# Four norm boundaries and an embedding stage, rebuilt around ScalarE evictions, pairs of tiles and squares kept off GpSimd

## The chip, the cores and the metric

The kernel runs on one core of a Trainium2 chip. The metric is the device time of one launch in microseconds (us), smaller is better. All tensors are float32; a product of float32 precision is made of three TensorE passes over operands that are split in a high and a low part.

## What is computed

Two blocks over 272 rows (16 meta rows and 256 tokens) and a model width of 2048: an attention layer and a pooling layer, then a second block with an RWKV-7 mixer beside a latent attention, a gated convolutional FFN and a gated embedding. Each sublayer ends in the same way, and this is the part that matters here:

```python
def rms_norm(x, g):
    xf = x.astype(jnp.float32)
    y = xf * lax.rsqrt(jnp.mean(xf * xf, axis=-1, keepdims=True) + RMS_EPS)
    return (y * g.astype(jnp.float32)).astype(x.dtype)
...
        h = h + rms_norm(y, post_norm_g[i])
...
        h = h + rms_norm_2(mix, post_mix_norm[i])
        u = rms_norm_2(h, pre_ffn_norm[i])
...
        h = h + rms_norm_2(f, post_ffn_norm[i])
        e = p[i] @ w_ple[i]
        h = h + rms_norm_2(jax.nn.sigmoid(h @ w_ple_gate[i]) * e, ple_norm[i])
```

The result drops the 16 meta rows, and after the pooling windows (up to 16 rows back) they are needed by nothing.

## The kernel before

Activations lie transposed in SBUF: 16 tiles of 128 channels by 256 or 272 rows (`h` the residual stream, `y` a sublayer's result, `xa` and `xb` the operands, each as a high and a low part). Weights come in 393 slots of 1 MB, four k-tiles by 512 columns each, through a ring of four raw buffers. Per slot SP issues one DMA once the slot four earlier is used (L229), ScalarE makes the high part in two halves (`split_hi`, L187), VectorE subtracts it for the low part (`split_lo`, L194), and TensorE runs 4 column tiles x 4 k-tiles x 3 passes = 48 matmuls (`products`, L210 to L212) into four PSUM banks. Four slots make a chunk of four output tiles; chunks go in turn to banks 0 to 3 and 4 to 7. The order of every engine's work is written out by hand: each engine runs one long queue, in order, with semaphore waits.

A *boundary* lies between an output projection (`attn_out`, `pool_out`, `mix_out`, 16 slots each, or the last four `down` slots of the FFN) and the projection that follows it. Before the change it goes so:

- In the projection (`y_stage_pe`, L309) VectorE copies each chunk of four tiles from PSUM to `y` (L331), ScalarE squares it (L323), VectorE adds the squares (L335).
- After the last chunk TensorE sums the squares over partitions with four matmuls by ones (`sum_squares`, L242), ScalarE takes the root (L249), VectorE the reciprocal (L691).
- `operands_dve` (L253) then goes through four groups of four tiles: y times the reciprocal (L258), four times h += gain * y (L261), four times the low part of the next operand (L271; L269 where no gain is applied). `operands_act` (L278) makes the high parts (L288, L286) in between, and GpSimd squares the new h and adds the squares up (`squares_pool`, L294, L300 to L304). Each group signals `x_ready`, which frees one slot of the next projection's first chunk (`first_chunk_pe`, L704). The weight splits of slots 2 and 3 stand behind groups 2 and 3.
- The second norm (of h, applied by scaling the results of the next projection) is summed by L242 behind the first chunk and rooted at once.

Boundary 1 is attn_out to pool_in, 2 is pool_out to rw_down, 3 is mix_out to the FFN. Boundary 4 is the FFN to ple_gate: there the two `ple` slots (the embedding, half a slot at a time) run between the FFN's last products and the gate's first, `e_taken` being ScalarE's evictions of them (L1829). The kernel ends with the norm of ple_gate's result (L1972 to L1978) and four output DMAs. In pool_in (32 slots at 272 columns), GpSimd forms the windowed means of each of four groups from the evictions of chunks 0 to 3 (L793 to L802) and ScalarE and VectorE wait for them in their queues between two weight splits (L759, L817).

## Time and profile before

| | us |
|---|---|
| median of 3 runs | 2834.61 (2830.41 to 2836.78) |
| the profiled execution | 2834.77, of which the trace spans 2833.0 |
| TensorE busy | 2597.2 (92% of the span) |
| VectorE busy | 1708.5 (60%) |
| ScalarE busy | 1134.5 (40%) |
| GpSimd busy | 214.4 (8%) |
| mean granted TensorE clock | 0.947 of full speed |
| granted clock from 957.5 to 959.5, after the wait in boundary 2 | 0.50 |
| the same from 989 to 991 | 1.00 |
| first pooling on GpSimd (L793 to L802) | 660.41 to 672.08, 11.7 us |

A row of a timeline gives start, duration, engine, source line, operation, tiles, shapes and count; in square brackets the idle time of that engine before it and who ended it. Consecutive instructions of one form are merged, with the duration of all of them. Matmuls overlap in the pipeline, so their own durations (0.28 us) are longer than their spacing (about 0.12 us); TensorE's time is best read from its idle gaps and from the spacing of what it releases.

### The profile page before, as it was taken

How to read it: one execution, taken by the hardware profiler on the slowest of the kernel's cores; microseconds unless marked ns; L12 is line 12 of the kernel's file. 1: busy time of each engine (PE TensorE's matmuls, PEld its weight loads, DVE VectorE, ACT ScalarE, POOL GpSimd, SP SyncE). 2: the span in 40 equal slices, each digit the busy share in tenths (PEclk: the TensorE clock that was granted, in tenths of full speed). 3: DMA queues.
4: the chain of work that ended last, by engine and by line, in shares of the span. 5: the costliest groups of instructions: out<-in, count | busy, mean ns of one | idle time of the engine just before them, and what ended most of it. 6: DMA issues, size and time to landing. Idle time of an engine off the chain costs nothing.

```text
span 2833.0 us, 52259 instructions
## 1 busy us (share of the span) xinstructions
PE 2597.2 (92%) x22498; PEld 2544.9 (90%) x22498; DVE 1708.5 (60%) x1909; ACT 1134.5 (40%) x1486; POOL 214.4 (8%) x117
## 2 busy tenths in 40 slices
PE   5999999879999787987998999998999999999986
PEld 5999999879999787886986999987999999999986
DVE  5565666566455786294363544558666666666664
ACT  3344445423344351241244333434444444444452
POOL 3000000014400231031000000002000000000000
PEclk9999999999999899798796999998999999999998
DMA  4444444334445341040140555553455555554442
GB/s 162 164 149 148 148 149 147 120 133 143 170 177 186 112 160 73 31 148 33 62 162 30 189 184 190 182 179 123 167 190 179 191 179 191 178 190 180 178 149 104
DMA packets 59618, 419.97 MB, mean 148 GB/s; under 512 B 6464, under 2 KB 8640, under 8 KB 9056
## 3 DMA queue, kind: packets, MB, share of 16 engines
q1 hardware_dynamic: 59280, 417.26, 41.0%
q8 instruction: 109, 1.79, 0.2%
q0 software_dynamic: 208, 0.75, 0.1%
q14 instruction: 21, 0.17, 0.0%
HBM read 415.89 MB, written 2.10 MB: 148 GB/s over the span
## 4 chain that ended last, share of the span: by engine, by line
PE 85%; DVE 10%; ACT 2%; POOL 1%; issue 1%; DMA 1%; SPq 0%; DVEq 0%; ACTq 0%; POOLq 0%
PE banks L210 25%; PE banks L212 25%; PE banks L211 25%; DVE xa_lo_sb L271 2%; DVE weights_lo_sb L194 2%; PE banks L242 1%; DVE h_sb L261 1%; PE banks L918 1%; PE banks L1006 1%; POOL rw_tile_sb L1159 1%; PE banks L996 1%; PE banks L1005 1%; DMA raw_weights_sb<-weights 1%; PE banks L1392 1%; PE banks L375 1%
## 5 line engine op out<-in xcount | busy, mean ns | idle before, releaser
L210 PE MATMUL banks<-xa_hi_sb,weights_hi_sb 128*128 128x256 f32 (+1 forms) x4800 | 1379.7, 287 | 80.0 <-DVE xa_lo_sb L271 29.9
L212 PE MATMUL banks<-xa_hi_sb,weights_lo_sb 128*128 128x256 f32 (+1 forms) x4800 | 1366.4, 285 | 0.0
L211 PE MATMUL banks<-xa_lo_sb,weights_hi_sb 128*128 128x256 f32 (+1 forms) x4800 | 1363.9, 284 | 0.0
L194 DVE TENSOR_TENSOR weights_lo_sb<-raw_weights_sb,weights_hi_sb 128x1024 fp32r<-128x1024 f32 x786 | 947.3, 1252 | 312.7 <-ACT weights_hi_sb L187 303.1
L187 ACT CAST weights_hi_sb<-raw_weights_sb 128x1024 fp32r<-128x1024 f32 x786 | 778.5, 1046 | 640.8 <-DMA raw_weights_sb<-weights 640.5
L210 PEld LDWEIGHTS banks<-xa_hi_sb,weights_hi_sb 128*128 128x128 f32 x4800 | 914.8, 191 | 88.5 <-issue 38.2
L211 PEld LDWEIGHTS banks<-xa_lo_sb,weights_hi_sb 128*128 128x128 f32 x4800 | 917.3, 191 | 0.5
L212 PEld LDWEIGHTS banks<-xa_hi_sb,weights_lo_sb 128*128 128x128 f32 x4800 | 915.1, 191 | 0.0
L210 PE MATMUL banks<-ff_hi_sb,weights_hi_sb 128*128 128x256 f32 x704 | 200.0, 284 | 2.7 <-DVE ff_lo_sb L1891 2.7
L211 PE MATMUL banks<-ff_lo_sb,weights_hi_sb 128*128 128x256 f32 x704 | 199.7, 284 | 0.0
L210 PE MATMUL banks<-xb_hi_sb,weights_hi_sb 128*128 128x256 f32 (+1 forms) x688 | 196.6, 286 | 2.7 <-DVE low_flat_sb L1517 1.3
L212 PE MATMUL banks<-ff_hi_sb,weights_lo_sb 128*128 128x256 f32 x704 | 198.0, 281 | 0.0
L212 PE MATMUL banks<-xb_hi_sb,weights_lo_sb 128*128 128x256 f32 (+1 forms) x688 | 196.0, 285 | 0.0
L211 PE MATMUL banks<-xb_lo_sb,weights_hi_sb 128*128 128x256 f32 (+1 forms) x688 | 195.7, 284 | 0.0
L210 PEld LDWEIGHTS banks<-ff_hi_sb,weights_hi_sb 128*128 128x128 f32 x704 | 132.4, 188 | 2.9 <-DVE ff_lo_sb L1891 2.9
L212 PEld LDWEIGHTS banks<-ff_hi_sb,weights_lo_sb 128*128 128x128 f32 x704 | 134.7, 191 | 0.0
L210 PEld LDWEIGHTS banks<-xb_hi_sb,weights_hi_sb 128*128 128x128 f32 x688 | 129.7, 189 | 3.6 <-DVE low_flat_sb L1517 1.5
L211 PEld LDWEIGHTS banks<-ff_lo_sb,weights_hi_sb 128*128 128x128 f32 x704 | 132.9, 189 | 0.0
L212 PEld LDWEIGHTS banks<-xb_hi_sb,weights_lo_sb 128*128 128x128 f32 x688 | 130.0, 189 | 0.0
L211 PEld LDWEIGHTS banks<-xb_lo_sb,weights_hi_sb 128*128 128x128 f32 x688 | 129.8, 189 | 0.1
L1917 DVE TENSOR_TENSOR y_sb<-y_sb,banks 128x1024 f32<-128x1024 f32 x40 | 48.9, 1222 | 47.6 <-PE banks L212 47.6
L271 DVE SCALAR_TENSOR_TENSOR xa_lo_sb<-h_sb,params_sb,xa_hi_sb 128x272 fp32r<-128x272 f32 (+1 forms) x64 | 66.9, 1107 | 0.4
(365 smaller groups left out, 2096.8 us busy)
## 6 DMA issues: line engine op xcount, KB each, us to landing
raw_weights_sb<-weights SPq DMA_DIRECT2D x393, 1024.0 KB, 4.8
h_sb<-h SPq DMA_DIRECT2D x1, 2176.0 KB, 8.6
out<-h_sb SPq DMA_DIRECT2D x4, 512.0 KB, 2.8
masks_sb<-consts_rw POOLq DMA_DIRECT2D x1, 352.0 KB, 4.8
params_sb<-params SPq DMA_DIRECT2D x1, 305.5 KB, 8.1
consts_first_sb<-consts_first SPq DMA_DIRECT2D x1, 304.0 KB, 9.2
ple_sb<-ple_in POOLq DMA_DIRECT2D x1, 256.0 KB, 3.0
consts_sb<-consts SPq DMA_DIRECT2D x1, 192.0 KB, 8.3
```

Source lines behind the costliest of these rows:

```text
L187: act.copy(c.w_hi[n % RAW][:, half], c.raw[n % RAW][:, half]).then_inc(c.sem("hi_done"), 1)
L194: dve.tensor_tensor(c.w_lo[n % RAW][:, half], c.raw[n % RAW][:, half], c.w_hi[n % RAW][:, half].bitcast(F32), ALU.subtract).then_inc(c.sem ...
L210: pe.matmul(out, w_hi[:, k, a], x_hi[:, tile, cols], start=begin, stop=False)
L211: pe.matmul(out, w_hi[:, k, a], x_lo[:, tile, cols], start=False, stop=False)
L212: done = pe.matmul(out, w_lo[:, k, a], x_hi[:, tile, cols], start=False, stop=end)
L242: m = pe.matmul(c.ps[:, bank, 0:n], c.const("ones"), acc[:, j, cols], start=j == 0, stop=j == 3)
L261: m = dve.scalar_tensor_tensor(out=c.h[:, k, cols], in0=t["tmp"][:, j, cols], scalar=c.param(g_post, k), in1=c.h[:, k, cols], op0=ALU.mult ...
L271: m = dve.scalar_tensor_tensor(out=c.xa[1][:, k, cols], in0=c.h[:, k, cols], scalar=c.param(g_pre, k), in1=c.xa[0][:, k, cols].bitcast(F32 ...
L375: m = pe.matmul(ps[0:b - a, 4 + comp, SCORES_AT[q]:SCORES_AT[q] + b], t["qk"][:, comp, a:b], t["qk"][:, 2 + comp, 0:b], start=True, stop=True)
L918: m = pe.matmul(ps[:, bank + j // 2, 256 * (j % 2):256 * (j % 2) + 256], ones, src[:, j, :], start=True, stop=True)
L996: m = pe.matmul(ps[at_[q], g, 64 * (u % 8):64 * (u % 8) + 64], t["lm"][at_[q], u, :], t["yy"][at_[q], u, :], start=True, stop=True)
L1917: dve.tensor_tensor(y, y, out(x), ALU.add).then_inc(S("down_taken"), 1)
```

## The change

Boundaries 1 to 4 and the end are rewritten. ScalarE instead of VectorE takes chunks out of PSUM, with the post-norm's gain applied in the same copy (`gained`), and squares straight from PSUM. The last chunk is taken by single tiles, each signalled by `tile_done` in the last slot; two of its six sum matmuls are put before that slot (`y_sums_begin_pe`). The boundary then runs over eight pairs of tiles: scale a pair, add it to h, high parts, low parts, and TensorE waits per half slot. The squares of the new h are ScalarE's, added up by VectorE (`h_squares_dve`) behind the first split of the following chunk and summed on TensorE after that chunk's first slot. The splits of the next projection's slots 2 and 3 stand earlier in both queues. GpSimd's squares go, except at the kernel's start. At boundary 4 the order of embedding evictions, root and splits on ScalarE changes. Pool_in's chunks 4 to 7, the group products and what follows them run on 256 rows instead of 272.

```diff
     for half in range(2):
         pe.wait_ge(c.sem("lo_done"), at(2 * n + half + 1, i, 2 * step))
+        if ready is not None:
+            pe.wait_ge(c.sem("x_ready"), ready + half + 1)
...
+            if each and half and j < 3:
+                done.then_inc(c.sem("tile_done"), 1)
     done.then_inc(c.sem("slot_used"), 1)
...
+def boundary_dve(c, dve, st, t, b, norm, cols, g_pre, splits):
+
+    dve.wait_ge(c.sem("root_done"), norm + 1)
+    st.did(dve.reciprocal(t["rs"][:, cols], t["sd"][:, cols]))
+    done = PAIRS * (b - 1)
+
+    def scaled(q):
+        yq = c.y[:, 2 * q:2 * q + 2, cols]
+        dve.tensor_tensor(yq, yq, wide(t["rs"][:, cols], 2), ALU.mult).then_inc(c.sem("y_scaled"), 1)
+
+    def updated(q):
+        hq = c.h[:, 2 * q:2 * q + 2, cols]
+        dve.wait_ge(c.sem("y_scaled"), done + q + 1)
+        dve.tensor_tensor(hq, hq, c.y[:, 2 * q:2 * q + 2, cols], ALU.add).then_inc(c.sem("h_ready"), 1)
+
+    def low(q):
+        dve.wait_ge(c.sem("x_hi_ready"), KT * b + 2 * q + 2)
+        pair = slice(2 * q, 2 * q + 2)
+        if g_pre is None:
+            m = dve.tensor_tensor(c.xa[1][:, pair, cols], c.h[:, pair, cols], c.xa[0][:, pair, cols].bitcast(F32), ALU.subtract)
+        else:
+            for k in range(2 * q, 2 * q + 2):
+                m = dve.scalar_tensor_tensor(out=c.xa[1][:, k, cols], in0=c.h[:, k, cols], scalar=c.param(g_pre, k),
+                                             in1=c.xa[0][:, k, cols].bitcast(F32), op0=ALU.mult, op1=ALU.subtract)
+        m.then_inc(c.sem("x_ready"), 1)
+
+    scaled(0)
+    updated(0)
+    for q in range(1, PAIRS):
+        scaled(q)
+        low(q - 1)
+        updated(q)
+        if q in splits:
+            split_lo(c, dve, splits[q])
+    low(PAIRS - 1)
+
...
+def h_squares_dve(c, dve, st, b, cols):
+
+    four = lambda g: c.y[:, 4 * g:4 * g + 4, cols]
+    for g in range(1, 4):
+        dve.wait_ge(c.sem("h_squared"), PAIRS * (b - 1) + 2 * g + 2)
+        st.did(dve.tensor_tensor(four(0), four(0), four(g), ALU.add))
+    dve.tensor_tensor(c.y[:, 0:2, cols], c.y[:, 0:2, cols], c.y[:, 2:4, cols], ALU.add).then_inc(c.sem("squares_ready"), 1)
+
+
+def boundary_act(c, act, b, cols, g_pre, splits):
+
+    for q in range(PAIRS):
+        act.wait_ge(c.sem("h_ready"), PAIRS * (b - 1) + q + 1)
+        for k in range(2 * q, 2 * q + 2):
+            if g_pre is None:
+                m = act.copy(c.xa[0][:, k, cols], c.h[:, k, cols])
+            else:
+                m = act.activation(c.xa[0][:, k, cols], c.h[:, k, cols], ACT.Copy, scale=c.param(g_pre, k))
+            m.then_inc(c.sem("x_hi_ready"), 1)
+        if g_pre is not None:
+            act.activation(c.y[:, 2 * q:2 * q + 2, cols], c.h[:, 2 * q:2 * q + 2, cols], ACT.Square).then_inc(c.sem("h_squared"), 1)
+        if q in splits:
+            split_hi(c, act, splits[q])
...
+def h_sums_pe(c, pe, cols, squares):
+
+    pe.wait_ge(c.sem("squares_ready"), squares)
+    for bank, a, part in spare(cols):
+        for j in range(2):
+            m = pe.matmul(c.ps[:, bank, a:a + part.stop - part.start], c.const("ones"), c.y[:, j, part], start=j == 0, stop=j == 1)
+    m.then_inc(c.sem("stats_done"), 1)
...
+def first_chunk_pe(c, pe, n0, x, b, cols):
+
+    for s in range(4):
+        products(c, pe, n0 + s, x, [(k, 4 * s + k) for k in range(4)], banks(c, 0, cols.stop - cols.start), cols,
+                 s == 0, s == 3, ready=x_before(b) + 2 * s)
...
+Y_SQUARED, Y_ADDED = 7, 3
+
+
+def y_sums_begin_pe(c, pe, t, base, cols, bank, a):
+
+    pe.wait_ge(c.sem("y_added"), Y_ADDED * (base // 4) + 3)
+    for j in range(2):
+        pe.matmul(c.ps[:, bank, a:a + cols.stop - cols.start], c.const("ones"), t["acc"][:, j, cols], start=j == 0, stop=False)
+
+
+def y_sums_end_pe(c, pe, t, base, cols, bank, a):
+
+    for j in range(4):
+        pe.wait_ge(c.sem("y_squared"), Y_SQUARED * (base // 4) + 3 + j + 1)
+        m = pe.matmul(c.ps[:, bank, a:a + cols.stop - cols.start], c.const("ones"), t["sq"][:, j, cols], start=False, stop=j == 3)
+    m.then_inc(c.sem("stats_done"), 1)
...
+            if chunk == s == 3:
+                pe.wait_ge(c.sem("y_taken"), base + 3)
+                y_sums_begin_pe(c, pe, t, base, cols, 0, 0)
...
+                     banks(c, chunk % 2, cols.stop - cols.start), cols, s == 0, s == 3,
+                     ready=None if ready is None or chunk else ready + 2 * s, each=chunk == s == 3)
+    y_sums_end_pe(c, pe, t, base, cols, 0, 0)
...
+def gained(c, act, chunk, j, cols, g_post, src):
+
+    k = 4 * chunk + j
+    return act.activation(c.y[:, k, cols], src, ACT.Copy, scale=c.param(g_post, k))
...
+    if chunk == 2:
+        act.wait_ge(c.sem("y_added"), Y_ADDED * (base // 4) + 1)
+    if chunk < 3:
+        act.wait_ge(c.sem("slot_used"), done)
+        act.activation((t["sq"] if chunk else t["acc"])[:, :, cols], c.ps[:, half:half + 4, 0:n], ACT.Square).then_inc(c.sem("y_squared"), 1)
+        for j in range(4):
+            m = gained(c, act, chunk, j, cols, g_post, bank(j))
+        m.then_inc(c.sem("y_taken"), 1)
+        return
+    act.wait_ge(c.sem("y_added"), Y_ADDED * (base // 4) + 2)
+    for j in range(4):
+        if j < 3:
+            act.wait_ge(c.sem("tile_done"), 3 * (base // 4) + j + 1)
+        else:
+            act.wait_ge(c.sem("slot_used"), done)
+        act.activation(t["sq"][:, j, cols], bank(j), ACT.Square).then_inc(c.sem("y_squared"), 1)
+        if j < 2:
+            gained(c, act, chunk, j, cols, g_post, bank(j))
+    for j in range(2, 4):
+        m = gained(c, act, chunk, j, cols, g_post, bank(j))
+    m.then_inc(c.sem("y_taken"), 1)
+
+
+def y_add_dve(c, dve, chunk, cols, base, t):
+
+    if chunk not in (1, 2):
+        return
+    count = Y_ADDED * (base // 4)
+    dve.wait_ge(c.sem("y_squared"), Y_SQUARED * (base // 4) + chunk + 1)
+    dve.tensor_tensor(t["acc"][:, :, cols], t["acc"][:, :, cols], t["sq"][:, :, cols], ALU.add).then_inc(c.sem("y_added"), 1)
+    dve.wait_ge(c.sem("y_added"), count + chunk)
+    if chunk == 2:
+        dve.tensor_tensor(t["acc"][:, 0:2, cols], t["acc"][:, 0:2, cols], t["acc"][:, 2:4, cols], ALU.add).then_inc(c.sem("y_added"), 1)
...
+        if n0 + m < N_SLOTS:
+            split(n0 + m)
         if m == 17:
             take(3, n0 + 16)
-        if n0 + m < N_SLOTS:
-            split(n0 + m)
-        if m % 4 == 1 and m < 17:
+        elif m % 4 == 1:
             take((m - 5) // 4, n0 + m - 1)
...
-        chunk(n0 + 12, 1, 2, i)
+            products(c, pe, n + s, c.xa, [(k, 4 * s + k) for k in range(4)], banks(c, half, cols.stop - cols.start), cols,
+                     s == 0, s == 3, i, 8)
+            if sums and s == 0:
+                h_sums_pe(c, pe, cols, 2)
+
+    chunk(n0 + 4, 1, None, R, sums=True)
+    chunk(n0 + 8, 0, 1, R)
+    chunk(n0 + 12, 1, 2, R)
+    with pe.Fori(0, 2) as i:
+        chunk(n0 + 16, 0, 3, BOTH, i)
+        chunk(n0 + 20, 1, 4, BOTH, i)
...
+    y_stage_split(c, lambda n: split_hi(c, act, n), lambda chunk, n: y_take_act(c, act, chunk, n, R, 0, t, "post0"), n0, 4)
+    root(c, act, 0, t["sd"], R, S("stats_done"), 2, S("root_done"))
+    split_hi(c, act, n0 + 18)
+    boundary_act(c, act, 1, R, "pre1", {1: n0 + 19})
...
 
     S = c.sem
     R = slice(0, ROWS)
-    squares_pool(c, pool, st, 1, R, t["acc"], t["sq"])
...
+        if m == 4:
+            h_squares_dve(c, dve, st, 1, R)
+        if m == 6:
             pre_root_dve(c, dve, st, t, 2, R)
-        if m % 4 == 1:
+        if m % 4 == 1 and m > 5 or m == 6:
             chunk = (m - 5) // 4
-            dve.wait_ge(S("slot_used"), n0 + m - 1)
+            dve.wait_ge(S("slot_used"), n0 + 4 * chunk + 4)
...
     masks, _ = columns(CONSTS_RW)
     mask = lambda name, k=16: wide(t["masks"][:, masks[name][0]:masks[name][1]], k)
     half = lambda x: ps[:, x:x + 2, :].rearrange("p b (j r) -> p (b j) r", j=2)
-    for m in range(4, 6):
-        split_lo(c, dve, n + m)
+    split_lo(c, dve, n + 4)
+    h_squares_dve(c, dve, st, 2, BOTH)
+    split_lo(c, dve, n + 5)
...
+        down(n, x, each=x == 3)
+    pe.wait_ge(S("tile_added"), 1)
+    y_sums_begin_pe(c, pe, t, 12, BOTH, 4, SEQ)
+    y_sums_end_pe(c, pe, t, 12, BOTH, 4, SEQ)
...
     pe.wait_ge(S("y_taken"), 15)
     ple(0, 0, 0)
     pe.wait_ge(S("y_taken"), 16)
+    pe.wait_ge(S("root_done"), 8)
     ple(0, 1, 1)
     pe.wait_ge(S("e_taken"), 1)
-    norm_between_pe(c, pe, t, 12, BOTH, 7)
+    ple(1, 0, 0)
     pe.wait_ge(S("e_taken"), 2)
-    ple(1, 0, 1)
-    pe.wait_ge(S("root_done"), 8)
-    ple(1, 1, 0)
+    ple(1, 1, 1)
     n = FIRST_SLOT["ple_gate"]
-    pe.wait_ge(S("e_taken"), 4)
-    y_stage_pe(c, pe, n, c.xa, BOTH, 16, lambda s: pe.wait_ge(S("x_ready"), 17 + s))
-    norm_between_pe(c, pe, t, 16, BOTH, 8)
+    pe.wait_ge(S("e_taken"), 3)
+    y_stage_pe(c, pe, t, n, c.xa, BOTH, 16, lambda s: pe.wait_ge(S("x_ready"), x_before(4) + 2 * s), ready=x_before(4))
...
+    for x in range(3):
         split_hi(c, act, n + 2 + x)
-        squares(x, 12)
+        taken(x)
+    split_hi(c, act, n + 5)
+    act.wait_ge(S("y_added"), Y_ADDED * 3 + 2)
+    for j in range(4):
+        if j < 3:
+            act.wait_ge(S("tile_added"), j + 1)
+        else:
+            act.wait_ge(S("y_taken"), 16)
+        act.activation(t["sq"][:, j, BOTH], c.y[:, 12 + j, BOTH], ACT.Square).then_inc(S("y_squared"), 1)
+    act.wait_ge(S("y_squared"), Y_SQUARED * 4)
+    for j in range(4):
+        gained(c, act, 3, j, BOTH, "post_ffn", c.y[:, 12 + j, BOTH]).then_inc(S("y_gained"), 1)
+    root(c, act, 4, t["sd"], BOTH, S("stats_done"), 8, S("root_done"), at=SEQ)
     n = FIRST_SLOT["ple"]
 
     def e_taken(x, half):
         act.wait_ge(S("slot_used" if x % 2 else "ple_done"), n + x // 2 + 1 if x % 2 else x // 2 + 1)
         act.copy(t["e"][:, 4 * x:4 * x + 4, :], c.ps[:, 4 * half:4 * half + 4, 0:SEQ]).then_inc(S("e_taken"), 1)
 
+    split_hi(c, act, n + 2)
     e_taken(0, 0)
+    split_hi(c, act, n + 3)
     e_taken(1, 1)
-    root(c, act, 0, t["sd"], BOTH, S("stats_done"), 8, S("root_done"))
-    e_taken(2, 1)
-    split_hi(c, act, n + 2)
-    e_taken(3, 0)
-    split_hi(c, act, n + 3)
+    boundary_act(c, act, 4, BOTH, None, {})
+    e_taken(2, 0)
...
-    for m in range(4, 6):
-        split_lo(c, dve, n + m)
+    split_lo(c, dve, n + 4)
+    h_squares_dve(c, dve, st, 3, BOTH)
+    split_lo(c, dve, n + 5)
+    split_lo(c, dve, n + 6)
     pre_root_dve(c, dve, st, t, 6, BOTH)
     dve.wait_ge(S("zeros"), 3)
     taken(0, 0, None, n + 4)
-    split_lo(c, dve, n + 6)
...
+    for x in range(3):
         split_lo(c, dve, n + 2 + x)
         dve.wait_ge(S("slot_used"), n + x + 1)
         y = c.y[:, 4 * x:4 * x + 4, BOTH]
         dve.tensor_tensor(y, y, out(x), ALU.add).then_inc(S("y_taken"), 1)
-        squares(x, 12)
+        y_add_dve(c, dve, x, BOTH, 12, t)
+    split_lo(c, dve, n + 5)
+    for j in range(4):
+        if j < 3:
+            dve.wait_ge(S("tile_done"), 3 * 3 + j + 1)
+        else:
+            dve.wait_ge(S("slot_used"), n + 4)
+        y = c.y[:, 12 + j, BOTH]
+        dve.tensor_tensor(y, y, ps[:, 4 + j, 0:SEQ], ALU.add).then_inc(S("tile_added" if j < 3 else "y_taken"), 1)
     n = FIRST_SLOT["ple"]
-    dve.wait_ge(S("root_done"), 8)
-    st.did(dve.reciprocal(t["rs"][:, BOTH], t["sd"][:, BOTH]))
     split_lo(c, dve, n + 2)
-    split_lo(c, dve, n + 3)
+    dve.wait_ge(S("y_gained"), KT)
+    boundary_dve(c, dve, st, t, 4, 7, BOTH, None, {3: n + 3})
...
+            else:
+                for j in range(4):
+                    y = c.y[:, 12 + j, BOTH]
+                    dve.wait_ge(S("ple_gated"), 3 + j + 1)
+                    dve.tensor_tensor(y, y, t["e"][:, 12 + j, :], ALU.mult).then_inc(S("tile_added"), 1)
+                    dve.wait_ge(S("tile_added"), 3 + j + 1)
+                    dve.tensor_tensor(t["sq"][:, j, BOTH], y, y, ALU.mult).then_inc(S("y_squared"), 1)
     dve.wait_ge(S("root_done"), 9)
...
+    done = 4 * PAIRS
+    for q in range(PAIRS + 1):
+        if q < PAIRS:
+            dve.wait_ge(S("y_gained"), KT + 2 * q + 2)
+            yq = c.y[:, 2 * q:2 * q + 2, BOTH]
+            dve.tensor_tensor(yq, yq, wide(t["rs"][:, BOTH], 2), ALU.mult).then_inc(S("y_scaled"), 1)
+        if q:
+            hq = c.h[:, 2 * q - 2:2 * q, BOTH]
+            dve.wait_ge(S("y_scaled"), done + q)
+            dve.tensor_tensor(hq, hq, c.y[:, 2 * q - 2:2 * q, BOTH], ALU.add).then_inc(S("out_ready"), 1)
```

## Rows read from the trace of the kernel before

**Rows 1.** TensorE's waits by releaser: us in total, times, longest.

```profile
PE banks L210 <- DVE xa_lo_sb L271: 29.9, 6, 9.2
```

**Rows 2.** The chain that ended last, boundaries 1 to 3: start, us, what.

```profile
601.46 1.30 DVE y_sb L331
...
654.78 1.83 PE banks L242 x8
...
940.35 1.24 DVE y_sb L331
...
991.82 1.73 PE banks L242 x8
...
1902.45 1.24 DVE y_sb L331
...
1952.09 1.73 PE banks L242 x8
```

**Rows 3.** TensorE's timeline at the first product of boundary 2.

```profile
955.96 0.58 PE L210 MATMUL banks<-xa_hi_sb,weights_hi_sb 128*128 128x256 f32 x1 [8.66 <-DVE xa_lo_sb L271]
```

**Rows 4.** VectorE's timeline in boundary 2.

```profile
947.85 1.75 DVE L691 RECIPROCAL rs_mid_sb<-sd_mid_sb 128x256 f32<-128x256 f32 x1 [1.54 <-ACT sd_mid_sb L249]
949.63 1.23 DVE L258 TENSOR_TENSOR tmp_sb<-y_sb,rs_mid_sb 128x1024 f32<-128x1024 f32 x1
950.89 1.67 DVE L261 SCALAR_TENSOR_TENSOR h_sb<-tmp_sb,params_sb,h_sb 128x256 f32<-128x256 f32 x4
...
958.79 5.46 DVE L271 SCALAR_TENSOR_TENSOR xa_lo_sb<-h_sb,params_sb,xa_hi_sb 128x256 fp32r<-128x256 f32 x4
...
972.46 2.35 DVE L194 TENSOR_TENSOR weights_lo_sb<-raw_weights_sb,weights_hi_sb 128x1024 fp32r<-128x1024 f32 x2
```

**Rows 5.** GpSimd's timeline in boundary 2, then GpSimd's and VectorE's at the kernel's start.

```profile
958.90 2.13 POOL L300 TENSOR_TENSOR sq_sb<-h_sb 128x1024 f32<-128x1024 f32 x1 [4.06 <-DVE h_sb L261]
...
24.59 3.35 POOL L304 TENSOR_TENSOR p_sb<-p_sb,a_sb 128x1088 f32<-128x1088 f32 x1
...
29.01 5.03 DVE L271 SCALAR_TENSOR_TENSOR xa_lo_sb<-h_sb,params_sb,xa_hi_sb 128x272 fp32r<-128x272 f32 x12
```

**Rows 6.** ScalarE's timeline: high parts of boundary 2, then boundary 4.

```profile
951.41 1.71 ACT L288 ACTIVATE xa_hi_sb<-h_sb,params_sb 128x256 fp32r<-128x256 f32 x4 [3.60 <-DVE h_sb L261]
...
2676.78 1.06 ACT L1820 ACTIVATE late_acc_sb<-y_sb 128x1024 f32<-128x1024 f32 x1 [6.68 <-DVE y_sb L1952]
2677.75 1.99 ACT L187 CAST weights_hi_sb<-raw_weights_sb 128x1024 fp32r<-128x1024 f32 x2
...
2699.60 1.28 ACT L249 ACT_TABLE_LOAD   x1
2700.89 0.48 ACT L249 ACTIVATE sd_sb<-banks,small_sb 128x256 f32<-128x256 f32 x1
```

**Rows 7.** VectorE's timeline in pool_in and at the first RWKV chunk.

```profile
750.69 1.29 DVE L817 TENSOR_TENSOR xb_lo_sb<-sq_sb,xb_hi_sb 128x1088 fp32r<-128x1088 f32 x1 [11.55 <-ACT xb_hi_sb L759]
...
777.66 1.29 DVE L830 TENSOR_TENSOR y_sb<-banks,rs_mid_sb 128x1088 f32<-128x1088 f32 x1 [3.72 <-PE banks L212]
...
801.85 1.29 DVE L830 TENSOR_TENSOR y_sb<-banks,rs_mid_sb 128x1088 f32<-128x1088 f32 x1 [3.68 <-PE banks L212]
...
1016.25 1.22 DVE L896 TENSOR_TENSOR y_sb<-banks,rs_sb 128x1024 f32<-128x1024 f32 x1 [1.89 <-PE banks L212]
```

**Rows 8.** VectorE's and TensorE's timeline at boundary 4.

```profile
2675.53 1.22 DVE L1952 TENSOR_TENSOR y_sb<-y_sb,banks 128x1024 f32<-128x1024 f32 x1 [2.94 <-PE banks L212]
...
2693.05 1.21 DVE L1952 TENSOR_TENSOR y_sb<-y_sb,banks 128x1024 f32<-128x1024 f32 x1
...
2714.80 0.55 PE L210 MATMUL banks<-xa_hi_sb,weights_hi_sb 128*128 128x256 f32 x1 [8.80 <-DVE xa_lo_sb L269]
```

**Rows 9.** ScalarE's timeline at the end, then VectorE's.

```profile
2807.43 1.02 ACT L1846 ACTIVATE y_sb<-banks 128x1024 f32<-128x1024 f32 x1 [15.39 <-PE banks L212]
...
2828.06 1.67 DVE L1978 SCALAR_TENSOR_TENSOR h_sb<-late_tmp_sb,params_sb,h_sb 128x256 f32<-128x256 f32 x4
```

313 lines of the change are left out of this document (136 added, 177 removed).

## The prediction

> **What bounds the kernel now.** The table comes first: TensorE is busy 92% of the span and no other engine over 60%, so what counts is where TensorE idles. The list of its waits names the place: its longest entry that the change touches is products that wait for the low part of an operand, L271, 29.9 us in six waits [rows 1]. They lie in boundaries 1 to 3. The chain of waits shows what one boundary costs: from the copy of the last chunk out of PSUM to the end of the second norm's sums, where the next projection's second chunk starts, pass 55.2, 53.2 and 51.4 us in boundaries 1, 2 and 3 [rows 2]. The work in it is one chunk: 24.2 us at 272 columns, the spacing of two evictions in pool_in [rows 7], and 22.5 us at 256, as from 991.82 + 1.73 to the next chunk's eviction at 1016.25 [rows 2, 7]. So each boundary holds some 30 us that are not products. They begin with 15.6 us before the first product of boundary 2 [rows 2, 3].
>
> In that stretch VectorE's rows show two kinds of time. Four updates of h (L261) take 1.67 us, four low parts (L271) of the same size 5.46 us [rows 4]. GpSimd squares h meanwhile [rows 5]. At the kernel's start, with GpSimd done at 27.94, twelve L271 at 272 columns take 5.03 us, 0.42 us each [rows 5]. So I take L271 alone at 0.42 us, and 1.37 beside GpSimd's squares.
>
> **Boundary 2, step by step** (0 is the copy's old start, 940.35; VectorE works at 1.23 us for four tiles, so 0.65 for a pair [rows 4]; ScalarE at 0.43 per tile [rows 6]). The last tile's square is ready at 0.5, its sum on TensorE at 1.8, as three of the four tail matmuls (0.43 each, 1.73 for four [rows 2]) wait for nothing. ScalarE copies the remaining tiles until 1.4 and then loads the root's table, 1.28 [rows 6], root at 3.2. Reciprocal (1.75 [rows 4]) 5.0; scale, add 6.4; two high parts 7.4; two low parts 8.3. First product at 8.4 instead of 15.6. From there a pair costs VectorE 0.65 (add) + 1.0 (ScalarE's high parts with two handovers, the next scale hidden in it) + 0.84 = 2.5 us, and TensorE 2.8 for its half slot. The two splits (2.35 each [rows 4]) cost VectorE about 3.2 net; TensorE has lead enough to lose only 1.4 of it. Then 22.5 of products and 1.5 for the clock, which is granted at half of full speed (1.2 of 2.4 GHz) for some 3 us after the idle time, as now (table): the second chunk starts at 8.4 + 22.5 + 1.5 + 1.4 = 33.8 instead of 53.2. Gain 19.4.
>
> What it gives back. Two sum matmuls now run before the last slot, two more inside the second chunk: 0.86 each time. The squares of h move to VectorE: three adds and a short one, 4.4 us behind the first split. Root and reciprocal come 6.7 us later than before relative to the second chunk. Behind them are queued the first shift, the split of the chunk's third slot (TensorE stalls 1.6 there), the angles and two more splits. VectorE then gets to the next eviction (before: 22.7 after the chunk's start, with 1.9 of slack [rows 7]) at 27.5, 4.8 late, and from there the chain runs over VectorE and GpSimd. Net of boundary 2: 19.4 - 0.9 - 4.8 = 13.7.
>
> **Boundary 1** by the same steps at 272 columns, no table load on the path (none stands there now): second chunk at 34.6, gain 20.6. Given back: 0.9 and 0.9 for sums. Its first eviction now waits for the later reciprocal, ends 12.2 after the chunk's start and only then releases GpSimd's pooling, for which ScalarE and VectorE wait in their queues before the split of slot 8. Pooling took 11.7 (table) and loses an instruction, I take 10.4; high and low part 2.3, half a split 1.2: the split is ready at 26.3, TensorE wants it at 25.1, stall 1.2. The fourth pooling ends in front of slot 20, today just in time (L817 ends at 751.98 [rows 7], chunk 5 starts at 753.2); with chunk 4 1.6 us shorter it costs 0.9. Net: 20.6 - 1.8 - 2.1 = 16.7.
>
> **Boundary 3**: second chunk at 33.8 instead of 51.4, gain 17.6. Back: 0.9 and 0.9 for sums, and 1.0 because the conv taps (later reciprocal) stand before the split of slot 7. Net 14.8. GpSimd's memset of y moves behind the sums and delays the first eviction to 12; it is hidden by chunk 2.
>
> **Pool gate.** 20 slots at 256 columns instead of 272: 24.2 against 22.5 for four [rows 7, 2], 0.41 a slot, TensorE being gapless there: -8.1. VectorE's group loop keeps up, since group 2 needs group 0 only.
>
> **Boundary 4** goes the other way. The FFN's last chunks are still added by VectorE, and now ScalarE multiplies each by its gain before the next split: add 1.3, square 1.1, four gains 1.7, split 2.0, then VectorE's low half 1.2, a period of 7.4 us [rows 4, 6] against TensorE's 5.7 for a slot. With the first add at 2675.5 [rows 8] the third ends at 2691.9, and the split of the second embedding slot stands before the single-tile adds: they start at 2698.2, while the products end at 2692.8, just ahead of today's last add [rows 8]. TensorE waits 5.8 us for the first of them and sums at half rate until 2703.2; gains, table load and root end at 2703.9. VectorE splits a slot (to 2707.3), takes the reciprocal (to 2709.1), and its first update of h ends at 2710.5. The products now wait for the third embedding eviction (`e_taken` 3), which is queued on ScalarE behind all eight pairs. So no pair overlaps a product: seven pairs at 2.25 (low part in one instruction, no square), 2.0 for a split and the last high parts end at 2729.2, the eviction at 2730.3, first gate product at 2730.4 against 2714.80 now [rows 8], where nothing stalls behind it either. Cost 15.6. The nearest rows bound it: 0 if the pairs overlapped as today, and 22 if the late adds came on top in full.
>
> **The end.** Now 25.6 us from the last eviction to the span's end, 22.3 of them until VectorE's last instruction at 2829.73 [rows 9]. After: last sigmoid 0.5, product and square 1.5, sum 2.3, root 2.9 (its table load hidden), reciprocal 4.7, sixteen pair operations of 0.65, 15.1. Gain 7.2, less 0.9 for the early sums: 6.4 rounded.
>
> **Sum.** 16.7 + 13.7 + 14.8 + 8.1 - 15.6 + 6.4 = 44.1. The profiled execution took 2834.77, the median is 2834.61: 2790.6.
>
> **A rule weighed.** The load of ScalarE's table took 1.28 us and the root began 0.01 us after it [rows 6]. The Trainium skill (ScalarE: Activation LUTs, What ACT_TABLE_LOAD costs) adds about 1.38 us of drain to each switch. By it the three switches on the path would take 4.1 us of the gain. The trace does not show it here, and the sum goes by the row.
>
> **Rivals.**
> 1. *A switch costs more than its row.* In boundaries 2, 3 and 4 the load is now on the path and nothing hides it. If it were twice its row, 3 x 1.3 are lost: 2794.5. Against it: root right behind the load [rows 6]. 6%. The rule above would put it so.
> 2. *The embedding boundary does overlap.* If the chain before it does not drift, or the eviction comes early, boundary 4 costs 0 to 5: 2777. Against it stands the queue order in the diff. 12%.
> 3. *The low parts stay slow*, because of the place (operands that ScalarE has just written) and not GpSimd. For it: 5.46 was measured at this place only; against it the 5.03 for twelve at the start, after ScalarE's writes too [rows 4, 5]. Then a pair costs 2.5 + 1.9 = 4.4 in boundaries 1 to 3, TensorE follows at that pace, 13 us lost in each: 2830. If the pairs of boundary 4 were slowed too by 1.9, 15 more are lost: 2845, slower than before. The point from which this decides is 1.6 us more per pair in all four. 4%.
> 4. *The splits fall behind.* ScalarE's four single copies per chunk come between weight splits in four projections. They are hidden by the ring (two slots, 11.3 us, are split ahead; the added work is 1.7). If that cover were gone, up to 1.7 x 12 = 20 come back: 2811. 6%.
> 5. *The change doesn't do what it says*: the second norm's root, late in all three places, sets new stalls beyond the 3.1 + 4.8 that I count. Twice as much: 2799. 12%.
>
> The forecast as it stands has 60%. Its own range is 2781 to 2801, from 3 us either way in each of three boundaries and 6 in boundary 4. To leave out no more than 2 in 10, I take in rivals 1, 2 and 5: 2775 to 2806. Within 0.2% of before (5.7 us, about what a measurement of this kernel can tell from no change) lie parts of rival 3 only.
> Faster 94%, same 3%, slower 3%.
>
> **What would show it.** L271's successor at 0.42 us a tile and no GpSimd work in boundaries 1 to 3: right on the cause. The chain from last product to second chunk of about 34 us in each. A TensorE gap before ple_gate of 13 to 16 us, released by ScalarE's embedding copy, and one of about 5.5 us before the FFN's sums. Stalls of 1 to 2 us at pool_in's slots 8 and 20, at the third slot of the first RWKV chunk, and of 1.0 at the FFN's slot 7. The prediction is wrong if the gate's gap is under 5 us, if pairs take over 2.9 us, or if new waits stand in the output projections.

## The result and the profile after

| | before | after |
|---|---|---|
| median, us | 2832.51 of 4 runs (2825.78 to 2836.78) | 2785.83 of 4 runs (2785.44 to 2786.22) |
| profiled execution, span | 2834.77, 2833.0 | 2786.22, 2784.4 |
| mean granted TensorE clock | 0.947 | 0.952 |
| VectorE, ScalarE, GpSimd busy | 1708.5, 1134.5, 214.4 | 1656.0, 1178.5, 163.0 |

The ratio is 0.9843, with an interval of 0.9824 to 0.9861: 46.7 us, 1.6% faster. The forecast was 2790.6, from 2775 to 2806.

TensorE's waits by releaser (total, times, longest), kernel after; they answer to [rows 1]:

```profile
PE banks L210 <- DVE xa_lo_sb L320: 18.9, 3, 6.5
PE banks L210 <- ACT e_sb L1957: 13.6, 1, 13.6
...
PE banks L210 <- DVE weights_lo_sb L194: 10.5, 6, 4.2
```

The 29.9 us for low parts are 18.9, one wait in each of boundaries 1 to 3; a new one of 13.6 stands at boundary 4. The waits for weight splits fell as well. The same view of the kernel before has:

```profile
PE banks L210 <- DVE weights_lo_sb L194: 25.2, 8, 4.2
```

Of these 25.2 us, 19.5 are six waits inside the first chunks of boundaries 1 to 3, two in each, and all six are gone. TensorE's timeline, kernel after, at all places that the prediction names:

```profile
610.19 0.57 PE L210 MATMUL banks<-xa_hi_sb,weights_hi_sb 128*128 128x272 f32 x1 [5.99 <-DVE xa_lo_sb L320]
...
733.39 0.39 PE L210 MATMUL banks<-xa_hi_sb,weights_hi_sb 128*128 128x256 f32 x1 [0.69 <-DVE weights_lo_sb L194]
...
923.34 0.55 PE L210 MATMUL banks<-xa_hi_sb,weights_hi_sb 128*128 128x256 f32 x1 [6.45 <-DVE xa_lo_sb L320]
...
953.79 1.02 PE L373 MATMUL banks<-y_sb,consts_sb 128*128 128x256 f32 x4
...
961.99 0.39 PE L210 MATMUL banks<-xa_hi_sb,weights_hi_sb 128*128 128x256 f32 x1 [1.54 <-DVE weights_lo_sb L194]
...
1870.86 0.55 PE L210 MATMUL banks<-xa_hi_sb,weights_hi_sb 128*128 128x256 f32 x1 [6.45 <-DVE xa_lo_sb L320]
...
1901.65 1.03 PE L373 MATMUL banks<-y_sb,consts_sb 128*128 128x256 f32 x4
...
1914.79 0.39 PE L210 MATMUL banks<-xa_hi_sb,weights_hi_sb 128*128 128x256 f32 x1 [0.83 <-DVE weights_lo_sb L194]
...
2611.06 0.58 PE L210 MATMUL banks<-ff_hi_sb,weights_hi_sb 128*128 128x256 f32 x1 [2.75 <-DVE ff_lo_sb L2035]
...
2642.23 2.08 PE L406 MATMUL banks<-late_acc_sb,consts_sb 128*128 128x256 f32 x4 [5.26 <-DVE y_sb L2100]
...
2672.89 0.58 PE L210 MATMUL banks<-xa_hi_sb,weights_hi_sb 128*128 128x256 f32 x1 [13.59 <-ACT e_sb L1957]
```

The first product of boundary 2 stood at 955.96 [rows 3], that of the gate at 2714.80 [rows 8]. L373 sums the squares of h one slot (5.66 us) into the second chunk, so that chunk starts at 948.1 and 1896.0. In boundary 1 the chain of waits of the kernel after has `642.40 1.18 PE banks L373 x8`; the chunk starts a slot of 272 columns (6.05) before it, at 636.35.

Where boundary 2 goes, ScalarE's and VectorE's timelines, kernel after (against [rows 4, 6]):

```profile
915.20 0.38 ACT L458 ACTIVATE sq_sb<-banks 128x256 f32<-128x256 f32 x1 [0.32 <-PE banks L212]
915.48 0.83 ACT L436 ACTIVATE y_sb<-banks,params_sb 128x256 f32<-128x256 f32 x2
916.33 1.28 ACT L251 ACT_TABLE_LOAD   x1
917.63 0.47 ACT L251 ACTIVATE sd_mid_sb<-banks,small_sb 128x256 f32<-128x256 f32 x1
...
922.32 0.88 DVE L320 SCALAR_TENSOR_TENSOR xa_lo_sb<-h_sb,params_sb,xa_hi_sb 128x256 fp32r<-128x256 f32 x2 [0.38 <-ACT xa_hi_sb L352]
...
924.77 0.88 DVE L320 SCALAR_TENSOR_TENSOR xa_lo_sb<-h_sb,params_sb,xa_hi_sb 128x256 fp32r<-128x256 f32 x2 [0.37 <-ACT xa_hi_sb L352]
```

Two low parts take 0.88 us instead of half of 5.46, and one pair follows another in 2.45 us. From the start of the last tile's square, straight from PSUM (915.20), 8.14 us pass to the first product and 32.9 to the second chunk.

The shift of the kernel after against the kernel before, stage by stage, adds up to the whole difference of the two profiled executions. The start of the last chunk's copy before [rows 2] answers to the last tile's square after (602.40, 915.20 and 1862.72 in boundaries 1 to 3). The last column is what the prediction let each step add to the shift; it adds up to its 44.1.

| point | before | after | shift so far | expected of this step |
|---|---|---|---|---|
| last copy, boundary 1 | 601.46 | 602.40 | +0.9 | +0.9 |
| second chunk of pool_in | 656.61 | 636.35 | -20.3 | -20.6 |
| last copy, boundary 2 | 940.35 | 915.20 | -25.2 | gate -8.1; +3.9 of sums and stalls |
| second chunk behind it | 993.55 | 948.1 | -45.5 | -19.4 |
| last copy, boundary 3 | 1902.45 | 1862.72 | -39.7 | +4.8, +0.9 |
| second chunk of the FFN | 1953.82 | 1896.0 | -57.8 | -17.6 |
| FFN's last down products | 2667.97 | 2611.06 | -56.9 | +1.9 |
| gate's first product | 2714.80 | 2672.89 | -41.9 | +15.6 |
| end of the span | 2833.0 | 2784.4 | -48.6 | -6.4 |

### The profile page after: what moved, and what is told of

Its sections match the earlier page's. It is cut to its first block, busy times and chain, and to the rows that moved or that the text cites. A ratio compares the mean times of both kernels' runs of the same rounds, so it can differ in the third digit from the quotient of the medians.

```text
span 2784.4 us, 52335 instructions
## 1 busy us (share of the span) xinstructions
PE 2580.3 (93%) x22510; PEld 2530.2 (91%) x22510; DVE 1656.0 (59%) x1891; ACT 1178.5 (42%) x1605; POOL 163.0 (6%) x92
## 3 DMA queue, kind: packets, MB, share of 16 engines
q8 instruction: 112, 1.84, 0.3%
## 4 chain that ended last, share of the span: by engine, by line
PE 85%; DVE 9%; ACT 3%; POOL 2%; issue 1%; DMA 0%; SPq 0%; DVEq 0%; ACTq 0%; POOLq 0%
PE banks L210 26%; PE banks L212 25%; PE banks L211 25%; DVE weights_lo_sb L194 3%; PE banks L1113 1%; PE banks L1024 1%; POOL rw_tile_sb L1265 1%; PE banks L1103 1%; PE banks L1112 1%; PE banks L1499 1%; PE banks L513 1%; PE banks L526 0%; PE banks L1498 0%; PE banks L1150 0%; PE banks L1161 0%
## 5 line engine op out<-in xcount | busy, mean ns | idle before, releaser
L210 PE MATMUL banks<-xa_hi_sb,weights_hi_sb 128*128 128x256 f32 (+1 forms) x4800 | 1374.2, 286 | 60.4 <-DVE xa_lo_sb L320 18.9
L2014 DVE TENSOR_TENSOR up_gate_sb<-banks,rs_sb 128x1024 f32<-128x1024 f32 x11 | 13.5, 1224 | 87.9 <-PE banks L212 86.3
```

Source lines behind the costliest of these rows:

```text
L210: pe.matmul(out, w_hi[:, k, a], x_hi[:, tile, cols], start=begin, stop=False)
```

## The experiments

Each starts from the kernel after unless it says otherwise. The runs of one kernel spread by up to 12 us here (15 in one case). A stretch of 900 us without any edit differs by up to 10 us between the profiled executions (last section), so small edits are read from their own stretch of the trace.

### GpSimd's squares put back (e1)

```diff
+    idle_squares_pool(c, pool, st, 2, BOTH, t["acc"], t["sq"])
...
+        pool.wait_ge(c.sem("h_ready"), PAIRS * (b - 1) + 2 * kg + 2)
+        st.did(pool.tensor_tensor((sq if kg else acc)[:, :, cols], hk, hk, ALU.mult))
+        if kg:
+            st.did(pool.tensor_tensor(acc[:, :, cols], acc[:, :, cols], sq[:, :, cols], ALU.add))
```

> The changed kernel with GpSimd's squares and adds of h put back at the first three boundaries, their result thrown away; nothing else waits for them. Theory (low parts are slow beside GpSimd): two low parts (L320, 0.88 us in the changed kernel) take 1.9 us more while GpSimd works, the pair's cycle goes from 2.45 to about 4.3 us against TensorE's 2.8 for half a slot, the four slots of the first chunk end 9 to 13 us later at each of the three boundaries: 27 to 39 us slower in all, near 2817. Rival (the slow low parts of the kernel before came from their place between updates, not from GpSimd): L320 stays at 0.88 us and the time within 2 us of 2785.8.

Measured: 2815.56 us, ratio to before 0.9932 (0.9908 to 0.9957), 29.7 slower than the kernel after. VectorE's and GpSimd's timeline in boundary 2:

```profile
940.89 0.87 DVE L320 SCALAR_TENSOR_TENSOR xa_lo_sb<-h_sb,params_sb,xa_hi_sb 128x256 fp32r<-128x256 f32 x2
...
942.51 2.21 POOL L340 TENSOR_TENSOR sq_sb<-h_sb 128x1024 f32<-128x1024 f32 x1 [5.69 <-DVE h_sb L311]
943.34 4.14 DVE L320 SCALAR_TENSOR_TENSOR xa_lo_sb<-h_sb,params_sb,xa_hi_sb 128x256 fp32r<-128x256 f32 x2 [0.38 <-ACT xa_hi_sb L362]
944.80 2.40 POOL L342 TENSOR_TENSOR acc_sb<-acc_sb,sq_sb 128x1024 f32<-128x1024 f32 x1
947.41 0.68 DVE L311 TENSOR_TENSOR h_sb<-h_sb,y_sb 128x512 f32<-128x512 f32 x1
```

The same two instructions, one pair later, take 4.14 us instead of 0.87 because they meet both GpSimd operations: they end at 947.48, the second of those at 947.20. So it is GpSimd and not the place, and rival 3 of the prediction is out. From TensorE's early sums to the second chunk, the three boundaries take 10.1, 11.1 and 9.3 us longer than in the kernel after: 30.5, which is all that the medians show.

### The kernel before without that load on GpSimd (e2)

```diff
+        cols = slice(cols.start, cols.start + 16) if b else cols
         hk = c.h[:, 4 * kg:4 * kg + 4, cols]
```

> The kernel before with GpSimd's squares of h cut to 16 columns at the first three boundaries (the second norm's sums are then of 16 columns only), all else as it was. Theory: the low parts of four tiles (L271, 5.46 us with GpSimd beside them) fall to about 1.7 us, four groups of them take 12 to 14 us out of VectorE's chain at each boundary, and the second chunk starts 10 to 14 us earlier: 30 to 42 us faster than the kernel before, near 2797, so that most of what the change brings is there without its other parts. Rival (the order by groups of four holds the boundary back, GpSimd is a side matter): 0 to 10 us faster.

Measured: 2791.97 us, ratio 0.9853 (0.9828 to 0.9878): the interval covers the 0.9843 of the whole change. Timelines of boundary 2 (against [rows 3 to 5]):

```profile
940.54 1.71 DVE L271 SCALAR_TENSOR_TENSOR xa_lo_sb<-h_sb,params_sb,xa_hi_sb 128x256 fp32r<-128x256 f32 x4
940.65 0.53 POOL L301 TENSOR_TENSOR acc_sb<-h_sb 128x64 f32<-128x64 f32 x1 [203.30 <-DVE h_sb L261]
...
942.31 0.58 PE L210 MATMUL banks<-xa_hi_sb,weights_hi_sb 128*128 128x256 f32 x1 [7.06 <-DVE xa_lo_sb L271]
```

Four low parts take 1.71 us instead of 5.46. The waits for weight splits behind the first product are gone too. In the kernel before TensorE's timeline has:

```profile
973.82 0.36 PE L210 MATMUL banks<-xa_hi_sb,weights_hi_sb 128*128 128x256 f32 x1 [3.61 <-DVE weights_lo_sb L194]
...
984.41 0.36 PE L210 MATMUL banks<-xa_hi_sb,weights_hi_sb 128*128 128x256 f32 x1 [3.18 <-DVE weights_lo_sb L194]
```

So these splits were late only because they stood behind the slow low parts in VectorE's queue. The gate's first product, 2714.80 before, came at 2670.76 here, 44.0 us earlier. Of these, 35.6 lie in the three boundaries, from TensorE's sums to the second chunk (12.8, 11.8 and 11.1). Another 6.3 lie in the stretch from boundary 2's second chunk to boundary 3's sums, 906.6 us instead of 912.9, which varies by more than that without any edit (last section). This kernel keeps groups of four, VectorE's copies and the gate's 272 columns. It also adds less than a full second norm needs, so I take 36 as the upper end for what leaving GpSimd brings, and the 30 that e1 gives back in the new order as the lower.

### The embedding copies moved inside (e3)

```diff
-    boundary_act(c, act, 4, BOTH, None, {})
-    e_taken(2, 0)
-    e_taken(3, 1)
+    boundary_act(c, act, 4, BOTH, None, {}, {0: lambda: e_taken(2, 0), 2: lambda: e_taken(3, 1)})
...
+        if q in after:
+            after[q]()
```

> The changed kernel with ScalarE's third and fourth copy of the embedding products moved from behind all eight pairs of the fourth boundary to behind its first and its third pair. Theory (the gate's first product waits 13.6 us for the third copy alone, and its operands have long been there): the gate starts 11 to 14 us earlier and all of it reaches the end, near 2773. Rival (the next wait takes its place: the raw weights of the gate's slots, which ScalarE waits 9.1 us for behind the stall): 0 to 5 us gained, near 2783.

Measured: 2772.56 us, ratio 0.9783 (0.9758 to 0.9807). The wait of 13.6 is gone; from the down products (2606.31) to the end (2768.6) pass 162.3 us instead of 173.3, so 11.0 of the 13.3 that the medians show lie in this stretch. The first slot of it has the same code in both and took 7.2 us instead of 8.5, at a granted clock of 0.81 over 8 us instead of 0.62, so the edit's own share is 9.7. Part of the wait is replaced. TensorE's timeline:

```profile
2668.03 0.55 PE L210 MATMUL banks<-xa_hi_sb,weights_hi_sb 128*128 128x256 f32 x1 [4.25 <-issue]
```

It stands ahead of the gate's third slot, whose split is queued behind all eight pairs on ScalarE (its high half starts at 2665.63) and VectorE. The rival named the right thing, the gate's weights, but what they wait for is their place in ScalarE's queue and not their transfer.

### The pool gate on 272 columns again (e4)

```diff
-        chunk(n0 + 16, 0, 3, BOTH, i)
-        chunk(n0 + 20, 1, 4, BOTH, i)
+        chunk(n0 + 16, 0, 3, R, i)
+        chunk(n0 + 20, 1, 4, R, i)
...
-            dve.tensor_tensor(out, ps[:, 4 * (chunk % 2):4 * (chunk % 2) + 4, 0:cols.stop - cols.start], wide(t["rs"][:, cols], 4),
+            dve.tensor_tensor(out, ps[:, 4 * (chunk % 2):4 * (chunk % 2) + 4, cols], wide(t["rs"][:, cols], 4),
```

> The changed kernel with the pool gate's products back on 272 columns (VectorE takes 256 of them as it does now). Theory (TensorE bounds that stretch, 768 products by 16 columns): 8.1 us slower, near 2794. Rival (that stretch is bound by the transfers of its weights): 0 to 2 us slower.

Measured: 2791.35 us (2786.56 to 2794.74), ratio 0.9851 (0.9825 to 0.9877), which by itself can't be told from the kernel after. The stretch can: from pool_in's first product to rw_down's pass 318.68 us (610.58 to 929.26) against 313.15. That is 5.5, less than the 8.1 I expected, since 16 slots are put back and not the four of the group products (4 x 0.41 less), and since the stall of 0.69 at slot 20 is not there when its chunk is longer. The term of the sum, 8.1 with a stall of 0.9 beside it, holds within 1 us.

### Boundary 4 in another order (e5)

The first embedding product stands ahead of the FFN's sums, the single-tile adds ahead of a split, the root ahead of the last gains, and copies and splits between the pairs:

```diff
+    e_taken(0, 0)
+    split_hi(c, act, n + 2)
+    boundary_act(c, act, 4, BOTH, None, {4: n + 4, 6: n + 5},
+                 {0: [lambda: e_taken(1, 1)],
+                  1: [last_gains, lambda: e_taken(2, 0), lambda: split_hi(c, act, n + 3)],
+                  3: [lambda: e_taken(3, 1)]})
...
+    boundary_dve(c, dve, st, t, 4, 7, BOTH, None, {1: n + 2, 3: n + 3, 5: n + 4}, gained=True)
```

> The changed kernel with its fourth boundary in another order: TensorE's first embedding product ahead of the FFN's sums, VectorE's single-tile adds ahead of the second embedding slot's split, the root ahead of the last four gains, the reciprocal ahead of the next split, the embedding copies between the pairs, and the splits of four slots between the pairs instead of behind them. Theory (that boundary is a matter of queue order): TensorE's wait of 5.3 us before the sums falls to under 1, the root is done 4 us earlier, and the gate's first product, at 2672.89 in the changed kernel, comes 17 to 21 us earlier; where moving the copies alone gave 13.3 us, this gives 4 to 8 more, near 2767. Rival (the low parts of the weights' split, 4 x 2.35 us between the pairs, become the bound of the gate's first chunk): new waits for L194 and L317 give half of it back, near 2771.

Measured: 2762.04 us, ratio 0.9755 (0.9728 to 0.9782). TensorE's timeline:

```profile
2637.54 1.03 PE L410 MATMUL banks<-late_acc_sb,consts_sb 128*128 128x256 f32 x4
2638.62 1.99 PE L417 MATMUL banks<-late_sq_sb,consts_sb 128*128 128x256 f32 x8
2641.37 0.36 PE L1851 MATMUL banks<-ple_hi_sb,weights_hi_sb 128*128 128x256 f32 x1 [0.76 <-issue]
...
2669.13 0.36 PE L210 MATMUL banks<-xa_hi_sb,weights_hi_sb 128*128 128x256 f32 x1 [1.96 <-issue]
```

The waits of 5.3 and 13.6 are gone, the sums run at full rate (1.03 for four instead of 2.08), and the gate starts at 2650.08, 41.2 us after the down products instead of 61.8. Of these 20.6 us 19.3 reach the end (154.0 from down products to end, 173.3 in the kernel after); the rest goes into the new wait of 1.96 before the gate's fourth slot. The first slot behind the down products' wait ran at the same clock in both (0.61 and 0.62 over 8 us). So order alone brings back more than the 15.0 that the change lost here.

### Narrower adds for the second norm (e6)

```diff
+    cols = slice(cols.start, cols.start + 16)
     four = lambda g: c.y[:, 4 * g:4 * g + 4, cols]
```

> The changed kernel with VectorE's four adds of h's squares cut to 16 columns at the first three boundaries (the second norm's sums are then of other numbers). Theory (the late second root costs 4.8 us at boundary 2, 1.0 at boundary 3 and nothing that shows at boundary 1): VectorE's 4.4 us leave the chain there, the stall at the third slot of the first RWKV chunk (1.54 us) goes, and 4 to 6 us are gained in all, near 2781. Rival (the root is late because of its place behind two splits and the sums' place in TensorE's queue, not because of the adds): the sums still run at the slot's end and under 2 us are gained.

Measured: 2785.30 us (2778.82 to 2787.29), ratio 0.9835 (0.9809 to 0.9862), no difference. ScalarE's timeline of the kernel after, then of this one:

```profile
954.85 0.48 ACT L381 ACTIVATE sd_sb<-banks,small_sb 128x256 f32<-128x256 f32 x1 [7.42 <-PE banks L373]
```

```profile
955.18 0.47 ACT L382 ACTIVATE sd_sb<-banks,small_sb 128x256 f32<-128x256 f32 x1 [7.44 <-PE banks L374]
```

The first products stand at 923.34 and 923.66, so the root comes 31.5 us behind them in both, and the stall of 1.54 stays, as the rival said. My attribution of the late root to VectorE's adds is wrong. That leaves the place of the sums in TensorE's own queue, behind a whole slot; e10 tries it.

### TensorE waits for four tiles (e7)

```diff
-            pe.wait_ge(c.sem("x_ready"), ready + half + 1)
+            pe.wait_ge(c.sem("x_ready"), ready + 2)
```

> The changed kernel with TensorE waiting for four tiles of the operand instead of two before it starts a slot of a boundary's first chunk; all other engines as they are. Theory (the hand-over by pairs lets TensorE start one pair, 2.45 us, earlier, and the rest of the chunk is TensorE's own pace): 2.5 us slower at each of boundaries 1 to 3 and nothing at the fourth, where the gate waits for another thing: 5 to 7.5 us slower, near 2792. Rival (TensorE waits for later pairs anyway): 0 to 2 us slower.

Measured: 2791.66 us, ratio 0.9860 (0.9834 to 0.9885), 5.8 slower. The wait at the first product grows from 5.99 to 8.54 in boundary 1 and from 6.45 to 8.91 in boundaries 2 and 3, by 2.5 each. By these waits TensorE's start after one pair is worth 7.5 us, one pair's time in each of three places; VectorE's own order by pairs is the same in both kernels and isn't tried here.

### The last chunk taken whole (e9)

```diff
-        if j < 3:
-            act.wait_ge(c.sem("tile_done"), 3 * (base // 4) + j + 1)
-        else:
-            act.wait_ge(c.sem("slot_used"), done)
+        act.wait_ge(c.sem("slot_used"), done)
```

> The changed kernel with ScalarE taking the four tiles of the last chunk of attn_out, pool_out and mix_out only once all of them are finished, with the same instructions. Theory (taking them by tile hides three squares and two gains beside the products): the last square, and so the root, comes 1.7 us later at each of boundaries 1 to 3, 5.1 us slower in all, near 2791. Rival (the table load and the sums hide it): 0 to 2 us slower.

Measured: 2791.31 us, ratio 0.9862 (0.9839 to 0.9884), 5.5 slower. From the early sums (L406) to the root pass 10.75 us in boundary 2 (911.42 to 922.17) instead of 9.14 (908.49 to 917.63), so the first product comes 1.6 us later. Boundary 3 shows the same 1.6 and boundary 1 shows 1.2: 4.4 in all.

### Sums inside the slot, table loaded early, fourth split early (e10)

On top of e5:

```diff
+        if half and between:
+            between()
...
+                     between=(lambda: h_sums_pe(c, pe, BOTH, 3)) if s == b == 0 else None)
...
+    act.activation(c.small[:, 2:3], c.eps["eps"], ACT.Sqrt, bias=c.eps["eps"], scale=1.0 / D)
     act.wait_ge(c.sem("y_added"), Y_ADDED * (base // 4) + 2)
...
-    boundary_act(c, act, 4, BOTH, None, {4: n + 4, 6: n + 5},
+    boundary_act(c, act, 4, BOTH, None, {4: n + 4, 5: n + 5},
```

> The kernel with the rebuilt fourth boundary and three more edits, each at a place of its own. First, TensorE sums h's squares between the two halves of the second chunk's first slot instead of behind that slot, at boundaries 1 to 3. If TensorE's queue is what makes the second norm's root late (narrower adds did not move it: root at 955.18 against 954.85), the root comes 2.3 us earlier against the boundary's first product, TensorE waits at most 0.6 us for the adds, and the stall of 1.54 us at the third slot of boundary 2's next chunk goes, as does that of 0.83 us in boundary 3's; if VectorE's queue is what makes it late, the root stays and the stalls too. Second, ScalarE takes a root of one constant column ahead of the last chunk's squares at boundaries 1 to 3, so that the root's table is loaded while it waits. In the changed kernel the load ends 0.7 us behind the sums at boundaries 2 and 3, so the first product there comes 0.7 us earlier (wait before it 5.8 instead of 6.45); by the rule that a switch costs a drain on top of its row it would be 2 us. Third, the split of the gate's fourth slot moves ahead of the last low parts: the stall of 1.96 us before that slot goes. Sum 4 to 6 us: near 2757. Rival: nothing of the first, 3 us in all, near 2759.

Measured: 2754.69 us (2745.51 to 2760.81), ratio 0.9723 (0.9699 to 0.9746), the fastest kernel here. TensorE's and ScalarE's timeline in boundary 2, then TensorE in boundary 3:

```profile
924.59 0.55 PE L212 MATMUL banks<-xa_hi_sb,weights_hi_sb 128*128 128x256 f32 x1 [5.75 <-DVE xa_lo_sb L324]
...
911.92 1.28 ACT L458 ACT_TABLE_LOAD   x1
...
918.88 0.47 ACT L253 ACTIVATE sd_mid_sb<-banks,small_sb 128x256 f32<-128x256 f32 x1 [0.61 <-PE banks L419]
...
953.82 0.47 ACT L387 ACTIVATE sd_sb<-banks,small_sb 128x256 f32<-128x256 f32 x1 [5.15 <-PE banks L379]
...
1869.63 0.55 PE L212 MATMUL banks<-xa_hi_sb,weights_hi_sb 128*128 128x256 f32 x1 [5.75 <-DVE xa_lo_sb L324]
```

The second root comes 29.2 us behind the first product instead of 31.5, and the stalls of 1.54 and 0.83 are gone: the place in TensorE's queue was their cause. The wait before the first product is 5.75 instead of 6.45, which is the 0.70 of the load and no more, and the root now waits 0.61 for the sums. The stall of 1.96 is gone. From down products to end pass 149.2 us, 4.8 less than in e5 where I expected 2. Of these, 1.3 are the first slot, whose code is the same (granted clock over 8 us 0.80 instead of 0.61). The other 3.5 lie behind the gate's first product: the stall of 1.96 and the clock, which in e5 stood at 0.50 for 3.4 us right behind the stall. The window from 2650 to 2673 of e5 had a granted clock of 0.93, the one from 2651 to 2674 of this kernel 1.00, so the small stall had cost the clock as well.

### GpSimd beside the fourth boundary (e11)

```diff
+            if q < 4:
                 m = dve.tensor_tensor(c.xa[1][:, pair, cols], c.h[:, pair, cols], c.xa[0][:, pair, cols].bitcast(F32), ALU.subtract)
+            else:
+                m = dve.scalar_tensor_tensor(out=c.xa[1][:, pair, cols], in0=c.h[:, pair, cols], scalar=1.0,
+                                             in1=c.xa[0][:, pair, cols].bitcast(F32), op0=ALU.mult, op1=ALU.subtract)
...
+        st.did(pool.tensor_tensor(tmp, hk, hk, ALU.mult))
+        m = pool.tensor_tensor(tmp, tmp, tmp, ALU.add)
...
+    dve.wait_ge(c.sem("squares_ready"), 5)
```

> The changed kernel with eight GpSimd operations (squares and adds of four tiles, result thrown away) beside the fourth boundary, and the low parts of that boundary's last four pairs made with scalar_tensor_tensor (gain 1.0) instead of tensor_tensor, same values. Theory (GpSimd and VectorE shut one another out only for some forms of instruction): the low parts by tensor_tensor (L317, 0.69 us a pair) and the adds stay within 0.05 us of their time while GpSimd works, and those by scalar_tensor_tensor take 2 to 4 us a pair instead of 0.88. Rival (any two-operand work of VectorE is slowed): both forms grow.

Measured: 2792.74 us, a single run. VectorE's and GpSimd's timeline:

```profile
2652.23 0.69 DVE L318 TENSOR_TENSOR xa_lo_sb<-h_sb,xa_hi_sb 128x512 fp32r<-128x512 f32 x1 [0.18 <-ACT xa_hi_sb L354]
...
2653.62 2.26 POOL L2012 TENSOR_TENSOR late_tmp_sb<-h_sb 128x1024 f32<-128x1024 f32 x1 [746.75 <-DVE h_sb L311]
2654.30 2.12 DVE L318 TENSOR_TENSOR xa_lo_sb<-h_sb,xa_hi_sb 128x512 fp32r<-128x512 f32 x1 [0.18 <-ACT xa_hi_sb L354]
2655.95 2.22 POOL L2013 TENSOR_TENSOR late_tmp_sb<-late_tmp_sb 128x1024 f32<-128x1024 f32 x1
2656.35 2.37 DVE L311 TENSOR_TENSOR h_sb<-h_sb,y_sb 128x512 f32<-128x512 f32 x1
...
2660.71 4.05 DVE L194 TENSOR_TENSOR weights_lo_sb<-raw_weights_sb,weights_hi_sb 128x1024 fp32r<-128x1024 f32 x2
...
2671.11 2.12 DVE L320 SCALAR_TENSOR_TENSOR xa_lo_sb<-h_sb,xa_hi_sb 128x512 fp32r<-128x512 f32 x1 [0.17 <-ACT xa_hi_sb L354]
```

My theory of the form falls: tensor_tensor goes from 0.69 to 2.12 and 2.37 just as scalar_tensor_tensor does, and a weight split from 2.35 to 4.05. The three short ones shown that are blocked end 0.5 us after the GpSimd operation that each of them met (2656.42 against 2655.88, 2658.72 against 2658.17, and 2673.23 against 2672.68).

## Why the prediction was right

- **The cause** (L271 at 0.42 us alone, 1.37 beside GpSimd): right. L320 is at 0.44 a tile, e1 brings the slow ones back and e2 takes them away. The price was a mean of something else, though: an instruction that meets no GpSimd operation keeps its time, and one that meets a running operation ends 0.28 us after it, whenever that is. The four low parts behind the 5.46 us took 0.48, 2.12, 2.62 and 0.48 (single instructions of the trace). In e1 two low parts took 4.14 or 2.06 us according to how many GpSimd operations they met. The sum does not hang on the 1.37, since it goes by 0.42; only rival 3 does.
- **Boundaries 1 to 3, to the second chunk**: first product at 8.4 (8.14 in boundaries 2 and 3), pair of 2.5 (2.45), second chunk at 34.6, 33.8 and 33.8 (34.0, 32.9 and 33.3). The table load was rightly placed in the sum, from 1.4 to 2.7 and so 0.9 behind the sums at 1.8; it ran from 1.1 to 2.4, 0.7 behind them, and e10 takes these 0.70 off the path. What was wrong is the count of three loads on the path, in rival 1 and in the rule weighed: in boundary 4 ScalarE has loaded before the sums come:

```profile
2645.38 1.28 ACT L251 ACT_TABLE_LOAD   x1
2647.76 0.47 ACT L251 ACTIVATE sd_sb<-banks,small_sb 128x256 f32<-128x256 f32 x1 [1.10 <-PE banks L413]
```

  Rival 1, a switch that costs twice its row, would have left 2.0 for e10 to win instead of 0.70. The Trainium skill (ScalarE: Activation LUTs, What ACT_TABLE_LOAD costs) adds a drain to each switch; no row here shows one, and the root began 0.02 us behind the load (917.63).
- **From the first product to the second chunk**, luck helped: two terms of boundaries 2 and 3 were off in opposite directions. The 1.4 for the splits did not come, since TensorE waits for nothing inside these chunks. The clock cost more than its 1.5: it stood at 0.50 until 927.5 and 1876.4, 4.2 and 5.5 us behind the first product, and the 192 products took 24.8 and 25.2 us instead of 22.5. The "some 3 us" had no row behind them: the kernel before has 0.50 until 961.5, 5.5 us behind its first product.
- **What is given back**: the 4.8 of boundary 2 show in the next 45 us. TensorE's first wait for GpSimd in RWKV ends 40.1 us behind the second chunk in the kernel before (1033.69) and 45.0 in the kernel after (993.08). The 870 us from there to boundary 3's last copy came out 0.9 longer, as summed, but that stretch varies by up to 10 us without any edit, so this agreement is luck. Stalls came of 1.54 (1.6 expected) at rw_down's third slot, 0.69 (0.9) at slot 20 and 0.83 (1.0) at the FFN's slot 7. The times were right and one reason wrong: "the squares of h move to VectorE" is not why the second root is late. TensorE's sums wait behind the second chunk's first slot (e6, e10). A further stall of 1.71 for a split (978.15), which the sum does not name, lies inside the same 45 us, and TensorE's wait for GpSimd behind it shrank from 3.41 to 1.84. None of TensorE's waits for splits stands in an output projection, so rival 4 is out.
- **The stall at pool_in's slot 8** (1.2 expected) did not come. Two terms were too high: the first eviction ends 11.1 us into the chunk, not 12.2, and GpSimd's pooling took 9.4, not 10.4:

```profile
646.17 1.29 DVE L936 TENSOR_TENSOR u_sb<-banks,rs_mid_sb 128x1088 f32<-128x1088 f32 x1
647.52 1.12 POOL L900 COPY sums_sb<-u_sb 128x4 f32<-128x4 f32 x1 [583.71 <-DVE u_sb L936]
...
654.54 2.41 POOL L906 TENSOR_TENSOR sq_sb<-sq_sb,u_sb 128x1024 f32<-128x1024 f32 x1
```

- **The pool gate**, 8.1: about right. The stretch from pool_in's second chunk to boundary 2's last copy is 4.9 us shorter (25.2 - 20.3); with the known costs in it (1.0 and 0.9 for sums, 0.7 of stall) the columns are worth 7.5, and e4 puts back 16 of 20 slots for 5.5.
- **Boundary 4**: 15.0 lost against 15.6, through the very chain that was written down: a period of 7.4 us, adds 5.3 late, the gate behind the third embedding copy for 13.6. Of the 15.0, 1.1 is the clock: the first slot behind the down products' wait took 8.5 us instead of 7.4 with the same code (0.62 over 8 us instead of 0.79). That both could be had back by order (e3, e5) was not in the prediction.
- **The end**: 6.7 against 6.4.
- **Not foreseen**: the FFN's loop ran 1.2 us shorter (55.7 to 56.9 in shift). The granted clock tells it, not the code. The same 113.8 us behind the loop's first stall, kernel before and kernel after, with the matmuls that fit in (x), then the clock in the third column from the right:

```profile
1986.20:2100.00 113.80, 113.78 (x940) 113.78 (x941) 69.58 (x76) 47.33 (x57) 0.00 (x0) 0.97 0.48 172
```

```profile
1930.50:2044.30 113.80, 113.74 (x950) 113.75 (x951) 70.04 (x77) 48.63 (x58) 0.00 (x0) 0.99 0.50 176
```

The balance, by the table of shifts: boundaries 1 to 3 gain 59.6 us up to the second chunk (21.2, 20.3 and 18.1), the gate 7.5, the end 6.7 and the FFN's loop 1.2; boundary 4 takes 15.0, and early sums, the late roots and the stalls take some 11. Of the 59.6, leaving GpSimd brings 30 (e1) to 36 (e2), TensorE's start after one pair 7.5 (e7), single tiles 4.4 (e9). The 12 to 17 that are left are ScalarE's evictions with the gain in the copy, VectorE's order by pairs and the earlier splits, which have no experiment of their own. These parts overlap, since a boundary in groups of four waits for other things than one in pairs; how the 59.6 split up exactly stays open between those ends.

## What to carry to other kernels

Before engines are given parallel work, look whether they can do it at once: a square on GpSimd that nobody was waiting for cost some 10 us in each boundary (e1), since VectorE's low parts could not end before it. When a helper with a fixed queue order is used again at a place with extra work (the embedding's copies and splits here), go through each engine's queue there and ask who waits for the last entry; two moved lines were worth some 10 us. A sum that must be early belongs between two halves of a slot of TensorE, not behind it, and a root's table can be loaded while ScalarE waits.

## What the runs showed of the hardware

A VectorE instruction with two inputs in SBUF that starts while a GpSimd tensor_tensor on SBUF runs does not end before it: 0.69 us of tensor_tensor became 2.12, ending 0.5 us behind GpSimd's, and two low parts of 0.87 became 4.14 behind two operations in a row. The Trainium skill (SBUF — State Buffer, Who interferes with whom) has the rule, that a VectorE instruction with two SBUF inputs contends with a GpSimd instruction that reads SBUF and that the later one blocks fully; e1 and e11 agree with it, and my expectation for e11, that tensor_tensor would be spared, does not.

A stretch with the same code varied more than most edits did. From TensorE's wait for GpSimd in RWKV (993.08 in the kernel after) to boundary 3's first product, kernel after and then e3, the granted clock is again the third column from the right:

```profile
993.10:1870.80 877.70, 787.24 (x8076) 758.29 (x8076) 469.52 (x503) 314.93 (x417) 68.47 (x35) 0.89 0.34 122
```

```profile
995.00:1865.80 870.80, 779.36 (x8076) 752.51 (x8077) 470.56 (x503) 314.99 (x417) 68.40 (x35) 0.90 0.35 123
```

8076 matmuls take 6.9 us less at a granted clock of 0.90 than at 0.89: of the longer stretch 189.0 us stood at half clock, of the shorter 174.6. Over the kernel after and e1, e3, e4, e5, e7, e9 and e11, whose code is the same there, the stretch from boundary 2's second chunk to boundary 3's early sums took 900.9 to 910.5 us. This is why medians of single edits are 3 to 5 us uncertain here, and why they were read from their own stretch.

A short stall can cost more than itself when the clock goes with it: with the 1.96 us before one slot of the gate gone and the clock in the 23 us around it at 1.00 instead of 0.93, e10 takes 109.2 us from the gate's first product to the end, 3.5 less than e5.
